# Second projection of a hybrid decoder step: order of its loads, where two stores are awaited, and where the first segment's keys are made

## The reference, cut to what matters

```python
h = einsum('btd,de->bte', x, w_in)            # 4096 columns: qa ka va ga | qb fb ib gb
# A: dilated sliding-window attention, 8 heads x 64, windows (128,1) (512,4) (2048,16),
#    for samples over a cache of 2048 keys and values; the shifted windows are outputs
# B: gated recurrence, 4 heads: f = lb + (1-lb)*sigmoid(fb); k = 1-f; q = silu(qb)
#    S_t = diag(f_t) S_(t-1) + k_t v_t^T ; o_t = S_t^T q_t ; final states are outputs
mix = concat([attn * silu(ga), norm(o_b) * silu(gb)])
y = layernorm(ALPHA * x + mix @ w_out)
```

## Time and profile before

| | us |
|---|---|
| three runs | 1641.53 median (1637.31 to 1641.63) |
| the profiled execution, its own time | 1639.29 |
| its span, first to last instruction | 1637.5 |
| PE busy | 1531.8 (94%) |
| DVE busy | 765.5 (47%) |
| ACT busy | 504.9 (31%) |
| POOL busy | 453.2 (28%) |
| mean granted TensorE clock | 0.955 of 2.4 GHz |

### The profile page before, as it was taken

One profiled execution on the slowest core, in us unless ns is written; L12 is line 12 of the kernel. 1 busy time (PEld: TensorE's weight loads), 2 busy tenths in 40 slices (PEclk: granted clock), 3 DMA queues, 4 the chain that ended last, 5 costly groups with the idle time before them and its releaser, 6 DMA issues. The chain is left out here.

```text
span 1637.5 us, 25532 instructions
## 1 busy us (share of the span) xinstructions
PE 1531.8 (94%) x9806; PEld 1371.3 (84%) x9806; DVE 765.5 (47%) x1938; ACT 504.9 (31%) x1426; POOL 453.2 (28%) x265
## 2 busy tenths in 40 slices
PE   7999999997799998999997999977999999599997
PEld 7999999994688776777776999967999999388885
DVE  6122200004322124122115789935777777488884
ACT  5111111112100113232212133244777777323221
POOL 1233300000240001000001000039776678345553
PEclk9999999997999999999997699988999999799999
DMA  9999995236856859776638168867688962856651
GB/s 306 332 333 350 352 291 149 78 123 197 238 168 202 284 194 305 247 264 220 215 110 204 30 215 273 250 146 145 131 201 188 198 157 78 280 194 229 206 181 52
DMA packets 176437, 340.50 MB, mean 208 GB/s; under 512 B 15651, under 2 KB 115299, under 8 KB 167459
## 3 DMA queue, kind: packets, MB, share of 16 engines
q1 hardware_dynamic: 144572, 173.70, 34.4%
q10 hardware_dynamic: 21248, 108.93, 20.9%
q0 software_dynamic: 10512, 56.48, 13.3%
HBM read 263.34 MB, written 156.48 MB: 256 GB/s over the span
## 5 line engine op out<-in xcount | busy, mean ns | idle before, releaser
L254 PE MATMUL acc<-xhi,whi 128*128 128x424 f32 (+1 forms) x640 | 227.1, 355 | 8.8 <-DVE xlo L233 8.8
L743 PE MATMUL nacc<-nwhi,nxhi 128*128 128x512 f32 (+1 forms) x544 | 219.2, 403 | 9.2 <-DVE nwlo L492 9.2
L254 PE MATMUL acc<-xlo,whi 128*128 128x424 f32 (+1 forms) x640 | 226.8, 354 | 0.0
L254 PE MATMUL acc<-xhi,wlo 128*128 128x424 f32 (+1 forms) x640 | 226.6, 354 | 0.0
L743 PE MATMUL nacc<-nwlo,nxhi 128*128 128x512 f32 (+1 forms) x544 | 214.4, 394 | 0.0
L743 PE MATMUL nacc<-nwhi,nxlo 128*128 128x512 f32 (+1 forms) x544 | 214.3, 394 | 0.0
L1340 ACT ACTIVATE a_prob<-a_prob,a_stage 128x256 f32<-128x256 f32 (+1 forms) x384 | 174.1, 454 | 98.8 <-DVE a_stage L1316 96.4
L1260 POOL CAST a_sorted<-a_plain 128x2048 fp32r<-128x2048 f32 x48 | 182.8, 3869 | 49.0 <-PE a_s_ps L1376 49.0
L1316 DVE CUSTOM_DVE_ANT_0 a_prob<-a_s_ps,a_bias 128x256 f32<-128x256 f32 (+1 forms) x384 | 125.5, 364 | 94.5 <-issue 62.6
L1400 PE MATMUL a_o_ps<-a_v,a_probT 128*128 128x64 f32 x1200 | 157.7, 269 | 0.2
L1400 PEld LDWEIGHTS a_o_ps<-a_v,a_probT 128*128 128x128 f32 x1200 | 149.9, 193 | 2.3 <-DVE a_probT L1327 1.6
(11 more groups left out here) (182 smaller groups left out, 2536.5 us busy)
## 6 DMA issues: line engine op xcount, KB each, us to landing
a_plain<-split_qk POOLq DMA_DIRECT2D x48, 512.0 KB, 11.5
out_kwin_s<-in_cache_kT ACTq DMA_DIRECT2D x8, 2048.0 KB, 19.7
split_qk<-spare POOLq DMA_DIRECT2D x16, 1024.0 KB, 14.3
spare<-in_xT SPq DMA_DIRECT2D x32, 512.0 KB, 7.5
projN<-nstage SPq DMA_DIRECT2D x32, 512.0 KB, 5.9
qg<-in_cache_kT ACTq DMA_DIRECT2D x8, 2048.0 KB, 11.1
d_vlow<-in_cache_v ACTq DMA_DIRECT2D x8, 2048.0 KB
out_kwin_s<-in_cache_kT ACTq DMA_DIRECT2D x8, 2032.0 KB, 28.8
```

Of the source, the lines that this page charges most:

```text
L254: mm = pe.matmul(acc[:, j, 0:n], w[:, u, k], x[:, k, c0:c0 + n], start=(k == 0 and a == 0), stop=(k == KD - 1 and a == 2))
L743: mm = pe.matmul(acc[0:m, n % 2], x[:, u, k, 0:m], w[:, k, g * H:(g + 1) * H], start=(k == 0 and b == 0), stop=(k == KD - 1 and b == 2))
```

## The change

It does six things.

1. SP no longer awaits the last two stores of stage 1 at its end. Their semaphores are handed to stage 2 as `stored_t`, where SP awaits them ahead of `load_recurrence` and POOL ahead of the key window's copies. `stage` moves to the low end of the memory so that nothing written early in stage 2 lies on it.
2. SP issues x tile 2 right behind w(1). `load_recurrence` loses the states, which are issued at n = 4, and w(2) is issued at n = 12. `bounds` waits for six loads, and `read_out` for the values and the states.
3. POOL awaits only `rep_d` before it loads `bias`. It issues `rep_p` later: once x tile 7 has been split (`x_split` at 8, DVE's step at n = 11), right ahead of the key window's copies.
4. `round_w(3)` on ACT moves behind the attention's `turn` of n = 33.
5. ACT makes the first segment's keys and factors in stage 2, at n = 61 to 64, one head of each per n (8 activations), into a new tile `kf`. Before that, `kf` holds `vec` and the cached values. Stage 3 makes only the second segment's at its start.
6. The last two stores of stage 2 are awaited in stage 3, by SP ahead of the load of v of segment 2, and by ACT behind `decays(1)`.

```diff
@@ project_transposed, SP @@
                 for u in range(2):
                     store(NCT - 2 + u, u, 0)
-                for u in range(2):
-                    sp.wait_ge(stage_free[u], 16 * (NCT // 2 + 1))
@@ project_natural, SP @@
                                      (sg[:], projT[12:16, :, T:TT].rearrange("h p t -> p h t")),
-                                     (S0[:], a["state"].rearrange("b h k v -> k b h v"))):
...
                 for k in range(KD):
                     load_w(1, k)
+                load_x(2)
+                for u in range(2):
+                    sp.wait_ge(stored_t[u], 16 * (NCT // 2 + 1))
                 load_recurrence()
-                for k in range(KD):
-                    load_w(2, k)
                 for n in range(NGR):
                     j = n // 2
+                    if n == HG + 1:
+                        sp.dma_start(S0[:], a["state"].rearrange("b h k v -> k b h v")).then_inc(hv_landed, 16)
+                    if n == 12:
+                        for k in range(KD):
+                            load_w(2, k)
                     if n % 2:
-                        if j + 2 < NTL * NPASS:
+                        if 2 < j + 2 < NTL * NPASS:
                             load_x(j + 2)
...
                 for u in range(2):
-                    sp.wait_ge(stage_free[u], 16 * NTL)
+                    sp.wait_ge(stage_free[u], 16 * (NTL - 1))
@@ project_natural, POOL @@
-                pool.dma_start(rep_p, bass.AP(...)).then_inc(b_repeated, 16)
                 nc.gpsimd.memset(qb[:], 0.0).then_inc(zeroed, 1)
                 nc.gpsimd.memset(bias[:], 0.0).then_inc(zeroed, 1)
                 pool.wait_ge(zeroed, 2)
-                pool.wait_ge(b_repeated, 32)
+                pool.wait_ge(b_repeated, 16)
                 for h in range(HA):
...
+                pool.wait_ge(x_split, 8)
+                pool.dma_start(rep_p, bass.AP(...)).then_inc(b_repeated, 16)
+                for u in range(2):
+                    pool.wait_ge(stored_t[u], 16 * (NCT // 2 + 1))
                 for c in range(NG):
                     pool.dma_start(kwin_p[c], projT[NG + c, :, 0:T]).then_inc(moved, 16)
@@ project_natural, DVE and PE @@
-                    dve.wait_ge(h_landed, 16 * 7)
+                    dve.wait_ge(h_landed, 16 * 6)
...
-                    pe.wait_ge(hv_landed, 16)
+                    pe.wait_ge(hv_landed, 32)
@@ project_natural, ACT @@
-                    if n == 2 * NTL - 1:
-                        for k in range(KD):
-                            round_w(3, k)
...
                     if c == 3:
                         act.wait_ge(t_done, 2 * s + 2)
                         turn(s, False, True)
+                    if n == 2 * NTL - 1:
+                        for k in range(KD):
+                            round_w(3, k)
+                    if LAST + EACH <= n < LAST + EACH + HB:
+                        h, (kd0, fd0) = n - LAST - EACH, (first["kf"][:, 0], first["kf"][:, 1])
+                        if h == 0:
+                            act.wait_ge(first["qk_landed"][0], 32)
+                            act.wait_ge(pv_done, NB)
+                        lb, oml, noml = (lbs_[:, m, h:h + 1] for m in (1, 2, 3))
+                        nc.scalar.activation(kd0[:, h], first["sg"][:, 0, h], ACT.Identity, bias=oml, scale=noml
+                                             ).then_inc(first["kd_done"], 1)
+                        nc.scalar.activation(fd0[:, h], first["sg"][:, 0, h], ACT.Identity, bias=lb, scale=oml
+                                             ).then_inc(first["fk_done"], 1)
@@ hgrn_prompt @@
                         load_segment(sp, projT, s, q, sg, qk_landed)
+                        for m in range(2):
+                            sp.wait_ge(first["stage_free"][m], 16 * (T // P + 1))
...
-                decays(0)
                 decays(1)
+                for u in range(2):
+                    act.wait_ge(first["stage_free"][u], 16 * (T // P + 1))
```

More of the change, by code:

```diff
@@ L142, in project_transposed @@
         sb, ps, sem = region(ctx, nc)
+        stage = sb("stage", [P, 2, TT])
         xhi, xlo = sb("xhi", [P, KD, TT], F32R), sb("xlo", [P, KD, TT], F32R)
@@ L146, in project_transposed @@
         whi, wlo = sb("whi", [P, 2, KD, P], F32R), sb("wlo", [P, 2, KD, P], F32R)
-        stage = sb("stage", [P, 2, TT])
         acc = ps("acc", [P, NCH, 512])
@@ L320, in project_natural @@
         bank = ps("sample_banks", [P, 6, 512])
-        stage_free = [sem(f"nstage_free{u}") for u in range(2)]
+        stage_free = first["stage_free"]
         w_hi, w_split, x_hi, x_split = sem("nw_hi"), sem("nw_split"), sem("nx_hi"), sem("nx_split")
@@ L347, in project_natural @@
             qem, host = sb("s_qem", [P, NB, HB, TS]), sb("s_ost", [TS, WB])
-            table, exp_sb, vec = sb("table", [BUCKETS + 1, HA]), sb("expand_sb", [BUCKETS + 1, NV]), sb("vec", [HA, NV])
+            table, exp_sb = sb("table", [BUCKETS + 1, HA]), sb("expand_sb", [BUCKETS + 1, NV])
+            vec = first["kf"][0:HA].rearrange("p a h t -> p (a h t)")[:, 0:NV]
         sb, _, _ = region(ctx, nc)
-        vlow, vhigh = sb("d_vlow", [P, NT, WA]), sb("d_vhigh", [P, NH // P, WA])
-        vn, prob = sb("d_vn", [NT, WA]), sb("d_prob", [P, NK])
+        vlow, vhigh = first["kf"][:].rearrange("p a h t -> p (a h t)").rearrange("p (r d) -> p r d", d=WA), sb("d_vhigh", [P, NH // P, WA])
+        prob, khigh = sb("d_prob", [P, NK]), sb("d_khigh", [P, 2, NG, NH])
+        vn, out, probT = sb("d_vn", [NT, WA]), sb("d_out", [P, 2, P]), sb("d_probT", [P, NKT, P])
         bias, ident = sb("d_bias", [P, WIN + NT]), sb("d_ident", [P, P])
@@ L896, in hgrn_prompt @@
         v = sb("v3", [P, 2, NCK, WB])
-        qd, kd, fd = (sb(n, [P, 2, HB, SEG]) for n in ("qd", "kd", "fd"))
+        qd, later = sb("qd", [P, 2, HB, SEG]), sb("kf1", [P, 2, HB, SEG])
+        S = sb("S", [P, 2, HB, DB])
+        kd, fd = ([first["kf"][:, m], later[:, m]] for m in range(2))
         at = sb("at", [P, 2, NG2, NCK * 2, CH])
         khn = sb("khn", [P, 2, NCK, WB])
-        S = sb("S", [P, 2, HB, DB])
         ost = sb("ost", [P, 2, NCK, WB])
@@ L906, in hgrn_prompt @@
         ost_free, state_kept = keep["ost_free"], keep["state_kept"]
-        zeroed, kd_done = sem("h_zeroed"), sem("h_kd_done")
-        fk_done, q1_done, a_done, upd_done, mask_done = (sem(f"h_{n}") for n in ("fk_done", "q1_done", "a_done", "upd_done", "mask_done"))
+        zeroed, kd_done, fk_done = sem("h_zeroed"), first["kd_done"], first["fk_done"]
+        q1_done, a_done, upd_done, mask_done = (sem(f"h_{n}") for n in ("q1_done", "a_done", "upd_done", "mask_done"))
         k_upd = sem("h_k_upd")
@@ L1005, in pair @@
                 def pair(tile, u, g, h):
-                    return tile[:, u, 2 * g:2 * g + 2].rearrange("p h t -> p (h t)").rearrange("p (n two j) -> p n two j", two=2, j=h)
+                    return (tile[u] if isinstance(tile, list) else tile[:, u])[:, 2 * g:2 * g + 2].rearrange("p h t -> p (h t)").rearrange("p (n two j) -> p n two j", two=2, j=h)
                 def first_products(s):
@@ L1092, in score @@
                         mm = pe.matmul(a_ps[:, i % 3, a * CH // 2:(a + 1) * CH // 2].rearrange("p (n j) -> p n j", j=w),
-                                       kd[:, u, h, t0:t0 + CH], late, start=True, stop=True)
+                                       kd[u][:, h, t0:t0 + CH], late, start=True, stop=True)
                     mm.then_inc(a_done, 1)
@@ L1741, in build @@
         copied = sem("win_copied")
+        stored_t = [sem(f"stage_free{u}") for u in range(2)]
         w_landed = [sem(f"nw_landed{k}") for k in range(KD)]
         x_landed = [sem(f"nx_landed{u}") for u in range(2)]
-        first = {"const": sem("h_const"), "qk_landed": [sem(f"h_qk_landed{u}") for u in range(2)]}
+        first = {"const": sem("h_const"), "kd_done": sem("h_kd_done"), "fk_done": sem("h_fk_done"),
+                 "stage_free": [sem(f"nstage_free{u}") for u in range(2)], "qk_landed": [sem(f"h_qk_landed{u}") for u in range(2)]}
         keep = {n: sem(f"k_{n}") for n in ("state_kept", "const", "ms_done", "rs_done", "half_set", "first_landed", "w_hi", "w_lo")}
```

45 lines of the change are left out of this document (22 added, 23 removed).

## The result

Five runs of the changed kernel have a median of 1658.27 us (1651.48 to 1659.36), five of the kernel before, taken beside them, 1641.15 (1637.31 to 1641.63). The ratio is 1.0094 with a 95% interval of 1.0068 to 1.0121: **slower by 17 us** by the medians, by some 15 by the ratio (two of the five runs took 1651.48 and 1652.30). The prediction said 1636, with a range of 1618 to 1645. It was wrong in sign, and the result lies outside the range.

The account below looks back on a forecast made before the run. PE, busy 94% of the span, was taken as the bound, with four standstills over 2 us. From 1639.3, -13.5 + 21.3 - 6.8 - 2.4 - 2.4 = -3.8 gave 1635.5; forecast 1636 us, range 1618 to 1645.

Parts of the forecast that it names:

- lead at group 7: Early stage 2: boundary 4.0, transpose wait 8.3 and slow group 1.7 saved, less 0.5 lateness; 13.5 us ahead.
- pile-up, to group 20: Groups 16 to 20: `rep_p`, w(2) and key window delay x tiles; the lead becomes 7.8 us late, costing 21.3.
- `round_w(3)`, group 35: Groups 33 to 35: L797 no longer waits behind w(3)'s roundings, values' matmuls start earlier; -6.8 us.
- stage 3 and after: Stage 3's start: stage begins 2.4 us earlier and DVE's products gain another 2.4 us.
- 2 MB at the 0.32 MB/us that SP's queue reached alone: Ahead of x tile 4: the states need 6.5 us, so the tile lands at about 431 to 434.
- cold group 7: Group 7 ran from 448.9 to 456.05 instead of 5.44 us; the excess 1.7 us was to vanish.
- The third link: Before group 20: x tile 10 alternates with ACT's first keys and lands at 545; group 20 at 547.2 instead of 539.40.
- Rival A: At group 16: x tile 8 gets past the key window, landing at 504.5; total 1621 us, chance 0.25.
- rival B: From 479 us: streams slow each other, x tile 8 lands at 529; total 1651 us, chance 0.12.
- rival C: Stage 1's boundary and stage 3's start give nothing, so 4.0 + 2.4 us are missing; 1641 us, chance 0.08.
- from there on PE had no wait until n = 33, so this stays: Behind group 20: the 7.8 us lateness persists, as PE had no wait until n = 33.
- from its first mask on DVE sets the pace: Stage 3: DVE's products start 3.5 us after the start instead of 5.90, and this is kept; -2.4 us.

Follow-up runs that it names:

- k7: k3 with POOL's eight bias loads also held until the fifth x tile is split; 1629.84 us, ratio 0.993.
- k3: The changed kernel with POOL waiting for 5 split x tiles instead of 8 before `rep_p` and the key window; 1636.88 us, ratio 0.9969.
- k10: k7 with `round_w(3)` back ahead of `turn`; 1627.48 us, ratio 0.9926.
- k4: The changed kernel with `round_w(3)` back ahead of `turn`; 1655.39 us, ratio 1.0087.
- k11: k7 with POOL's copy of the value window held until 28 x tiles are split; 1619.99 us, ratio 0.9873.
- k9: k7 with the first segment's keys and decays made at the start of stage 3 again; 1627.15 us, ratio 0.9925.
- k12: k11 with the first segment's keys and decays made at the start of stage 3 again; 1620.48 us, ratio 0.9883.
- k1: The changed kernel with `rep_p` issued right behind `rep_d` again, both awaited before the bias loads; 1646.43 us, ratio 1.0045.
- k2: The changed kernel with w(2) loaded ahead of the groups again, behind `load_recurrence`; 1647.74 us, ratio 1.005.

## Why the prediction was wrong

By its own steps, on the profiled executions, forecast and measured:

| step | forecast | measured |
|---|---|---|
| lead at group 7 | -13.5 | -4.5 |
| pile-up, to group 20 | +21.3 | +19.3 |
| sample's first scores late, group 22 | 0 | +2.4 |
| `round_w(3)`, group 35 | -6.8 | -6.1 |
| given back ahead of group 40 | 0 | +7.1 |
| stage 3 and after | -4.8 | +0.6 |
| sum | -3.8 | +19.0 |

(The rows of the table add up to +18.8; 0.2 is groups 36 to 39.)

**The lead at group 7 was mis-sized by 9 us.** In the prediction's terms, 4.0 + 8.3 + 1.7 - 0.5 = 13.5 came as 1.8 + 2.3 + 0.4 = 4.5. The failed step is "2 MB at the 0.32 MB/us that SP's queue reached alone", which carries 6.8 of the 9.0: the wait stayed at 5.96, and the "cold group 7" with it. The queue was not alone. The prediction took `rep_p` out of the way and did not ask what POOL would issue next. POOL, no longer held by `rep_p`'s landing, sent its eight bias loads in the same microsecond as the states. They are only 0.5 MB; by k7 they cost 7.0 us. The other 2.2 are the boundary, whose 4.0 was worth 3.2 at PE's first matmul and 1.8 at group 6.

**The pile-up: two links of three were right, and the sum in part by luck.** The split of x tile 8 was forecast 38.2 us behind group 11's evacuation (514 against 475.8) and came 37.35 behind it; the next tile was to be 16.4 later (530.4 against 514) and came 17.3 later. The chain (split, updates, states' store, x tile 9) is the one that the prediction wrote down. In offsets, the forecast steps at groups 16, 18 and 20 were 11.8, 5.5 and 4.0. Measured were 13.5, 5.8 and 0. The third link, x tile 10 beside the keys, did not exist: ACT's keys went out at 535.53 and not "5 us later than the 523.09", and the tile was ahead of them. (Its "17 us beside them" was also more than the prediction's own prices give, 64 x (0.16 + 0.04) = 12.8.) In its place came a term that the sum did not have, the low clock behind each standstill, 2.4 + 1.9 us. The waits alone, 11.0 and 3.9, were under the forecast. So 19.3 is near 21.3 because errors of both signs offset each other. k3 gives the price of the whole by itself: 21.4 us for one constant. Packet by packet is what the queues did here as well: from 508 to 512 us 295 packets of q0 and 295 of q1, from 512 to 516 us 383 and 386, and over the whole stretch from 486 to 520 us

```profile
q0 software_dynamic: 2046, 7.87, 63.8%
q1 hardware_dynamic: 2410, 3.49, 35.6%
```

so SP's queue moved 3.49 MB while POOL's moved 7.87. Rival A, by which x tile 8 gets past in a few turns, did not happen. The Trainium skill, in "DMA: Bandwidth & Descriptors", section "Queues, rings and completion order", states that an engine drains a whole packet of some 9 to 17 descriptors from one ring before it switches; the 295 to 295 of this trace do not agree with the uneven share that the prediction drew from that for rival A. Nor did rival B, by which the streams slow each other down: its tile 8 would have come 53 us behind group 11. The kernel was slower without it, because the lead that should have paid for most of the pile-up was not there. Every case hung on that lead, and but for the 4.0 us of rival C none had a price for its absence. That is where the range was too narrow.

**The rounding: gain right, its end wrong.** -6.1 came against -6.8. The failed step is "from there on PE had no wait until n = 33, so this stays", carried on behind n = 33 without asking. POOL's copy of the value window starts on the landing of a store whose group is finished ahead of the gain; x tile 20 is issued behind it. So a gain between the two only brings them nearer to each other, from 14.1 us apart in k10, without the gain, to 7.7 in k7 with it (7.8 after), and the tile lands when the copy lets it. k4 and k10 (no gain, no loss) and k11 (gain, no loss) show it from both sides.

**Stage 3.** The earlier start (2.4) and the earlier products (2.4) both stand in the trace as forecast. What failed is "from its first mask on DVE sets the pace": it did not, since PE's 64-column scores ran at the low clock from the beginning and DVE waited for them. The second half of rival C, with 0.08, had this; its first half, the boundary, was wrong. k9 and k12 show that early keys are worth nothing. The earlier start of the stage is kept to the end of the first segment's scores (2.5 us in k12) and is gone at stage 4. Why the segments between take it back is open.

Of what the prediction costed at nothing, two things cost time. One is the low clock behind a standstill, above. The other is x tile 11: SP issues it 16.1 us later than before (545.77 against 529.68) with groups that are 14.8 later, and it lands 1.1 us more slowly. DVE's `d_qb` stands behind its split, and PE idles 2.7 us ahead of the sample's first scores. In before, k1, k2, k3 and after alike PE starts these 0.7 us after that copy begins, so the wait is for it. Late keys are not the reason: they went out 12.4 us later (535.53 against 523.09), less than the groups.

## What to carry to other kernels

Where a transfer is taken out of the way, look at what its queue sends instead: every instruction that stood behind the removed wait now starts earlier, and small loads count. A gain is kept only if both sides of the next meeting move with it; where a copy's start is tied to an event ahead of the gain and a tile's issue to one behind it, the gain only brings them together, and the copy must move too (here one constant, 28 for 0, kept 7.5 us). A standstill of PE has to be priced with the groups at the low clock behind it: here 1.9 to 2.7 us for each wait of 3.9 to 11.0. Large copies that nobody awaits belong where the DMA share is low just before them, not at the same event as the next weights: 5 for 8 in one wait was 21 us.

## What the runs showed of the hardware

Small loads can disturb a neighbouring queue more than their bytes say: beside 0.36 MB of the bias loads, at 24.0% of the engines' time, SP's queue moved 1.06 MB less in 8 us. It gave up a quarter of its time (105.6% to 79.2%) and 45% of its bytes. The loads go into 8 partitions each; whether that is the reason no run shows, since none spreads them wider.

Two queues with packets of unequal size sent as many packets each: 295 and 295 from 508 to 512 us, where POOL's queue moved 1.08 MB and SP's 0.15.

TensorE can stay at the low clock, 1.2 GHz, while its rows show no idle time at all. In k11 the stretches from 860 to 900 us have PE busy 10.00 of 10.00 us at a granted 0.50, with 64-column matmuls at 49 in 10 us. These end at 903.55 and matmuls of 128 columns follow; from 905 to 910 the granted clock is 0.66, and 1.00 from 910. In the kernel with the keys in stage 3 (k9) the same narrow scores have a granted 1.00 from 865 to 870 us, and 0.50 from 875 to 910.
